# Stick-breaking pairs between softmax pairs, and their transposes ahead of the next scores

## What is computed

```python
h = rms_norm(x, norm_mix[i])
(q_n, kc, vc, ks_, vs_, kw, vw, g_n, q_s, k_s, v_s, q_f, k_f, v_f, f_l) = split_columns(h @ w_in[i])
o_nsa = nsa_mixer(...)                  # 8 heads: gated sum of a compressed, a selected and a window attention
o_sb = stick_breaking_attention(...)    # 4 heads
o_fox = forgetting_attention(...)       # 4 heads
x = x + concatenate([o_nsa, o_sb, o_fox]) @ w_out[i]
```

```python
log_beta = log_sigmoid(z)                        # z: scaled scores
log_1m = where(strict, log_beta - z, 0.0)        # = -softplus(z)
excl = cumsum(log_1m, reverse=True) - log_1m
a = where(strict, exp(log_beta + excl), 0.0)
```

## Time and profile before

| | |
|---|---|
| time, median of 3 runs | 1760.79 us (1760.14 to 1761.63) |
| the profiled execution's own time | 1762.81 us |
| its span, first to last instruction | 1760.9 us |
| mean granted clock of PE | 0.98 of full speed |
| busy: PE, PEld | 1672.1 us (95%), 1536.6 us (87%) |
| busy: DVE, ACT, POOL | 1108.6 us (63%), 821.4 us (47%), 47.5 us (3%) |
| chain that ended last, by engine | PE 78%, DVE 10%, ACT 6%, issue 4% |
| HBM read | 291.48 MB, 166 GB/s over the span |

### The profile page before, as it was taken

The page is one execution under the profiler, slowest core; times in us unless marked ns, Lnnn a source line. Parts: engine busy times, 40 slices in busy tenths (PEclk is TensorE's granted clock), DMA queues, the critical chain, the costliest instruction groups (busy, mean ns, idle before and its releaser), DMA issues.

```text
span 1760.9 us, 36950 instructions
## 1 busy us (share of the span) xinstructions
PE 1672.1 (95%) x12555; PEld 1536.6 (87%) x12570; DVE 1108.6 (63%) x1647; ACT 821.4 (47%) x1388; POOL 47.5 (3%) x45
## 2 busy tenths in 40 slices
PE   9989899999998989999899999799999999999998
PEld 7977779998897768999779888589899989989998
DVE  4555678887956457888757523358655574665544
ACT  5556556654355556664354322023544344454433
POOL 2000000000400000000000000200000000000000
PEclk9999999999999999999999999899999999999999
DMA  8430325567554023558818632108455764445551
GB/s 318 144 120 1 120 96 188 180 216 262 208 188 135 33 88 114 184 180 294 315 62 315 241 122 83 60 25 332 152 184 179 239 214 164 163 139 179 181 188 60
DMA packets 81009, 293.47 MB, mean 167 GB/s; under 512 B 9008, under 2 KB 10544, under 8 KB 80176
## 3 DMA queue, kind: packets, MB, share of 16 engines
q1 hardware_dynamic: 78768, 283.29, 47.3%
q10 hardware_dynamic: 2176, 9.27, 1.5%
HBM read 291.48 MB, written 1.05 MB: 166 GB/s over the span
## 4 chain that ended last, share of the span: by engine, by line
PE 78%; DVE 10%; ACT 6%; issue 4%; DVEq 1%; POOL 0%; SPq 0%; DMA 0%; ACTq 0%; POOLq 0%
PE projs L1362 51%; PE accs L1362 21%; PE ob L1362 4%; ACT WH L450 3%; DVE WL L824 2%; DVE rstd L911 1%; PE projs L1551 1%; DVE cprod L832 1%; DVE ring L834 1%; ACT scr L494 1%; DVE scr L917 1%; DVE AL L926 1%; ACT AH L512 0%; DVE x L848 0%; DMA ring<-in_stream 0%
## 5 line engine op out<-in xcount | busy, mean ns | idle before, releaser
L824 DVE TENSOR_TENSOR WL<-ring,WH 128x1024 fp32r<-128x1024 f32 x436 | 537.8, 1235 | 479.7 <-ACT WH L450 478.7
L450 ACT ACTIVATE WH<-ring 128x1024 fp32r (+1 forms) x436 | 460.8, 1057 | 617.9 <-PE projs L1362 394.4
L1362 PE MATMUL projs<-AH,WH 128*128 128x256 f32 (+1 forms) x2432 | 628.8, 296 | 28.9 <-ACT AH L512 9.6
L1362 PE MATMUL projs<-AL,WH 128*128 128x256 f32 (+1 forms) x2432 | 630.7, 296 | 1.3
L1362 PEld LDWEIGHTS projs<-AH,WH 128*128 128x128 f32 x2432 | 463.9, 193 | 45.6 <-issue 19.4
L1362 PEld LDWEIGHTS projs<-AL,WH 128*128 128x128 f32 x2432 | 463.3, 193 | 22.5 <-DVE AL L924 7.1
L1362 PE MATMUL projs<-AH,WL 128*128 128x256 f32 (+1 forms) x2432 | 362.1, 292 | 0.0
L1362 PEld LDWEIGHTS projs<-AH,WL 128*128 128x128 f32 x2432 | 326.5, 193 | 7.5
L1362 PE MATMUL accs<-FH,WH 128*128 (+1 forms) x768 | 187.2, 280 | 0.3
L1362 PE MATMUL accs<-FL,WH 128*128 (+1 forms) x768 | 186.6, 279 | 0.0
L1362 PEld LDWEIGHTS accs<-FH,WH 128*128 128x128 f32 x768 | 144.3, 188 | 1.2 <-issue 1.2
(11 more groups left out here) (216 smaller groups left out, 1509.6 us busy)
## 6 DMA issues: line engine op xcount, KB each, us to landing
ring<-in_stream SPq DMA_DIRECT2D x532, 512.0 KB, 3.4
W1v<-in_w ACTq DMA_DIRECT2D x2, 1024.0 KB, 6.2
W1k<-in_w ACTq DMA_DIRECT2D x2, 1024.0 KB, 9.8
D<-in_decay ACTq DMA_DIRECT2D x4, 512.0 KB, 3.3
x<-in_xT SPq DMA_DIRECT2D x2, 512.0 KB, 4.9
memT<-in_memT SPq DMA_DIRECT2D x1, 1024.0 KB, 11.1
ctxT<-in_ctxT ACTq DMA_DIRECT2D x1, 1024.0 KB, 7.5
out_y<-ybuf SPq DMA_DIRECT2D x8, 128.0 KB, 2.0
```

The costliest lines, as they stand in the source:

```text
L450: A(WH[:, s, :], ring[:, r % RING, :], ACT.Copy).then_inc(wh_ready, 1)
L824: V.tensor_tensor(WL[:, s, :], ring[:, r % RING, :], WH[:, s, :].bitcast(F32), ALU.subtract).then_inc(consumed, 1)
L1362: return T.matmul(out, lhsT, rhs, start=start, stop=stop, skip_group_check=True)
```

## The change

The list of units gets another order: soft 0 to 3 (blocks 0 and 1), stick block 4, soft block 2 twice, stick block 5, soft block 3 twice, fox blocks 6 and 7. In PE's loop a stick unit's `turn(v)` now goes ahead of `scores(v + 2)`, and `scores(v)` whose bank held a stick unit waits for that unit's `turned_copy` (the semaphore `pt_ready`) in place of the exponentials. The lists of ACT, DVE and POOL follow the new order of units by the same loops as before; the second attention (two "full" units) has no stick unit and keeps its order.

```diff
             out += [dict(kind="fox", b=6 + o, q=6 + o, k=13 + o, v=8 + 2 * o, gate=None, first=True, h=2 * o) for o in range(2)]
-            out += [dict(kind="stick", b=4 + o, q=4 + o, k=11 + o, v=4 + 2 * o, gate=None, first=True) for o in range(2)]
-            return finish(out)
+            stick = [dict(kind="stick", b=4 + o, q=4 + o, k=11 + o, v=4 + 2 * o, gate=None, first=True) for o in range(2)]
+            return finish(out[:4] + stick[:1] + out[4:6] + stick[1:] + out[6:])
...
                     if v >= 2:
-                        pe.wait_ge(exp_ready, softs[v - 2])
+                        if units[v - 2]["kind"] == "stick":
+                            pe.wait_ge(pt_ready, u - 1)
+                        else:
+                            pe.wait_ge(exp_ready, softs[v - 2])
...
                 for v in range(U):
-                    if v + 2 < U:
+                    stick = units[v]["kind"] == "stick"
+                    if v + 2 < U and not stick:
                         scores(v + 2)
                     turn(v)
+                    if v + 2 < U and stick:
+                        scores(v + 2)
                     if v:
                         values(v - 1)
```

## The result

The changed kernel took 1768.51 us (median of 6 runs, 1767.72 to 1770.50) against 1761.59 of the kernel before (6 runs, 1760.14 to 1762.06): a ratio of 1.0043, 95% interval 1.0030 to 1.0056, so 5.3 to 9.9 us slower, 7.6 by the ratio. Timed again on another chip it gave 1.0041 (1.0025 to 1.0056). The forecast was 9.1 slower with a range of 1766.5 to 1773.5.

The account below looks back on a forecast made before the run. PE was taken to bound the kernel; per layer, new waits of 8.05 us less the old 3.48 gave +4.57, +9.1 in both, so the median goes from 1760.8 to 1769.9 us, range 1766.5 to 1773.5.

Parts of the forecast that it names:

- What bounds: TensorE (PE), busy 95% of the span; the change was worth what it did to PE's waits, alike in both layers.
- Gaps A and D: PE's waits before turn(4) and turn(7), the stick products, for the chain ACT, DVE, GpSimd: 1.58 us each.
- Gaps B and E: PE's waits before scores(6) and scores(9) for the stick's exponential copy on ACT: 1.06 us each, bounds 0.91 to 1.06.
- Gap C: PE's wait before turn(5), as DVE's second(5) stands behind first(6), which waits for the late scores(6): 1.18 us.
- The end: PE's three waits after scores(11): before turn(10) 1.04 us, before turn(11) 0.28, for the last copy 0.27.
- The sum: New gaps of 8.05 us less the old 3.48: +4.57 per layer, +9.1 in both.
- the last step: The +4.57 us per layer counted for both layers as +9.1, with nothing in the long stages taking it up.
- Rival 1: Sticks hidden by PE's cover after all, faster: 1757.0 us, or 1753.8 with the end hidden as well; chance 0.08.
- A to E together: PE's five waits from before turn(4) to before scores(9), per layer: 6.46 us; below 1.89 the change would gain.
- Rival 2: PE's granted clock falls once per layer, costing 1.7 us each, in all +12.5: 1773.3 us; chance 0.07.
- Rival 3: Wait before turn(5) goes, those before turn(4) and turn(7) shrink: +1.89 us per layer, in all 1764.6; chance 0.05.

Follow-up runs that it names:

- both edits: The changed kernel with values(v-1) between a stick's product and the next scores, and DVE's second(v+1) ahead of first(v+2): stretch 40.55 us, ratio to before 1.0037.

## Why the prediction was right, and where not

- **What bounds.** Right: PE's busy time in the stretch the same to 0.14, the loss in waits, the two layers alike to a few hundredths.
- **Gaps A and D**, forecast 1.58 each: 1.63 each by the slots (136.87 + 0.80 to 139.30; the same before 152.68). That they are the uncovered end of the chain ACT, DVE, POOL is shown by the cut left out (0.85 each). That the late start of the chain is ACT's order is read from its rows only (Abs at 134.99 right behind an output); no run here changed it in the changed kernel.
- **Gaps B and E**, forecast 1.06: by the slots 142.44 - (139.30 + 2.18) = 0.96 and 155.82 - (152.68 + 2.18) = 0.96. The copy releases scores a tenth sooner than it releases values, inside the bounds of 0.91 to 1.06. That the queued values, put into this wait, would gain nothing behind the first stick but 0.8 behind the second, I had not said; the runs of values between and of both edits show it.
- **Gap C**, forecast 1.18: 1.09 by the slots (144.43 + 0.85 to 146.37), and shown by the run with DVE's order changed. No such gap behind stick 7: right.
- **The end**, forecast 1.04 + 0.28 + 0.27: 0.97, 0.26 and 0.27 by the slots. The last matmul of the stretch ends at 174.46.
- **The sum** over a stretch, forecast +4.57: +4.51. That this is so close is in part errors that cancel. The gaps by slots sum to 7.77, 0.28 less than the forecast's; but the scores of units 6 and 9 took slots of 1.19 and 1.18 (142.44 to 143.63, 155.82 to 157.00) where I had 1.10, and one gap of the kernel before was 0.13, not 0.18, as the transposes behind it took 0.80 (156.19 to 156.99), not 0.75. In the whole, forecast +9.1, the two ratios give 7.6 and 7.2, with 9.1 still inside both intervals. What looks too large is the last step, where I doubled the stretch and let nothing else change. The stretch before isn't 37.82 each time: in half of its six profiled instances it was 1.06 longer, while the four of the changed kernel were 42.3 each time. On average that makes 9.0 - 1.1 = 7.9 (an estimate from ten stretches). The other part is the time between the stretches: 394.6, 394.7 and 394.6 in the three profiles of before, 391.8 and 393.2 in the two of the changed kernel, and 391.8 to 395.8 over the others. The difference goes with the mean granted clock in the last 110 us of it (0.92 against 0.95 in the rows above). Why the changed kernel's was higher in both profiles is open: the three of before agree too well to call it chance, two profiles are few, and the run with the whole shifted couldn't tell.
- **Rival 1** (hidden after all) fell: A to E together are 6.27 by the slots, not below 1.89, and with 2.7 us more of cover behind each stick the stretch still took 42.7. The Trainium skill, "Perfetto Trace Analysis", section "Optimization Strategy", says that interleaving regimes may help; here the measured 42.33 for 37.82 decides against it.
- **Rival 2** (the clock falls) did not come true, but my evidence against it was wrong. I took one profile in which a wait of 2.25 left the clock at 1.00 as the rule; behind the same wait it dropped in three of six. The price was off as well: a fall behind that wait cost 1.06, where I had put 1.7. What kept the changed kernel clear of it in four stretches is likely that its waits are shorter, 1.56 at most by the brackets. That the fall is caused by the wait is argued from its place each time and from the filled wait, not proven. The Trainium skill, "TensorE: Matmul & The Clock Gate", section "A second HAM failure mode", tells of a kernel whose clock swung with frequent short idles of TensorE; here six waits of 0.9 to 1.6 us in each of four stretches left it at 1.00, so these traces don't show it.
- **Rival 3** (the gaps partly close) did not come true either: all eight gaps stood there, each within 0.1 of the forecast.

## What to carry to other kernels

In a pipeline of two banks like this one, a unit that keeps its bank until its last step holds back the scores of two units later, and with them everything that the other engines have queued behind those: count its cost as a drained and refilled pipeline, not as its own wait. At the end of a stage the pipeline drains anyway, and of the orders run here the one with the long chains there was cheapest: 37.82 against 41.57, 42.33 and 42.71. Before moving a unit, write down each engine's list around it and ask for every waiting instruction what stands behind it, ready; slots from the trace then gave the new gaps to a tenth of a microsecond here, and to two tenths in the order with the forgetting units.

## What the runs showed of the hardware that was not expected

The granted clock of PE fell behind waits of about two microseconds in some executions and not in others, with identical instructions: behind 2.18 us in three of six stretches of the kernel before and both of the shifted one, behind 2.71 in one of two, and behind 1.81 in one of two:

```profile
580.23 0.87 PE L1554 MATMUL projs<-const,scr 128*128 128x128 f32 x6 [1.81 <-DVE scr L975]
581.04 1.42 PE L1362 MATMUL ob<-PT,Vt 128*64 128x256 f32 x8
```

(second layer of the kernel with values between, 42.58 in place of 41.52: the values took 1.42 in place of 0.87). In the fourteen stretches whose longest wait was between 1.01 and 1.56 (the changed kernel's four, and two each with DVE's order changed, both edits, the cut left out, the forgetting unit behind, and the stick passes ahead of an output) it never did. Each fall cost 1.1 us here, 2.5 behind the longest wait. So a wait of two microseconds cost more here on average than its length, and one profile need not show it.
